# Experts of a hybrid decoder: token transposes moved behind the product transposes, and one filler matmul per pair of experts

## The chip, the cores and the metric

The kernel runs on one core of one Trainium2 chip. The metric is the device time of one execution in microseconds (us), and lower is better. Everything is float32.

## The reference, cut to what matters

The program is one inference step of a two-layer trunk with 320 tokens (256 of a prompt, 64 of a sample) of width 1024. Layer 0 mixes tokens with a Mamba-2 scan, layer 1 with latent attention. Behind either mixer stands the same mixture of experts, and the change lies in that alone. Each token goes to 2 of 32 experts, and each expert is a SwiGLU of width 256:

```python
for g in range(MOE_GROUPS):
    sl = slice(g * EXPERTS_PER_GROUP, (g + 1) * EXPERTS_PER_GROUP)
    hg = jax.nn.silu(jnp.einsum('nd,edf->nef', xt, w_gate[sl])) * jnp.einsum('nd,edf->nef', xt, w_up[sl])
    hg = hg * gate[:, sl, None].astype(hg.dtype)
    out = out + jnp.einsum('nef,efd->nd', hg, w_down[sl], preferred_element_type=jnp.float32)
```

The kernel computes each expert only for the tokens routed to it, and applies the two weights of a token afterwards.

## The kernel before

**Pairs.** The 32 experts of a layer are worked on as 16 pairs (`PAIRS`), numbered by j. Each expert has 64 slots for tokens, so a pair fills 128 rows. If an expert has more than 64 tokens, the whole loop over pairs would run again (a "window"); here it runs once a layer.

**One pair, step by step.** GpSimd gathers the 128 token rows of pair j from DRAM (`gather`, L1208). TensorE transposes them, 8 blocks of 128x128, into two PSUM banks (`turn`, L1072). ScalarE copies the first four blocks to SBUF (`rows_in` of ScalarE, L1158) and VectorE the other four (`rows_in` of VectorE, L1399). TensorE multiplies them with the gate and up weights of both experts (`gate_up`, L1086: 32 matmuls of 64 output rows, the two experts side by side). ScalarE takes SiLU of the gate half (`silu`, L1164), and VectorE multiplies it with the up half (`hidden`, L1406). TensorE transposes that product (`turn_hidden`, L1096, two blocks), VectorE copies it to `hT` (`hidden_turned`, L1411), and TensorE multiplies it with the down weights (`down`, L1111: 16 matmuls). ScalarE and VectorE copy the result out (L1170, L1417), and GpSimd scatters it to DRAM (`scatter`, L1216).

**The order on TensorE** is written out by hand and runs ahead of itself. Turn j of the loop holds filler matmuls, `gate_up(j + 1)`, `turn(w, j + 2)`, `turn_hidden(j)` and `down(j)`. The filler is `idle_work(n, bank)` (L1013): n matmuls of a constant 128x512 block that nobody reads. In the rows of a trace a float32 matmul counts as two records.

**The order on VectorE** follows it: in turn j, `hidden(j + 1)`, `rows_in(j + 2)`, `hidden_turned(j)`, `rows_out(w, j)`. An engine works its own list strictly in order, so an instruction that waits for a semaphore holds up all behind it.

**The weights.** A pair has 6 MB of weights, and there are six slots of one expert each (`RING`; in the trace four are called `ring` and two `hi`), so three pairs. SyncE issues all these loads into one DMA queue: gate and up weights of a pair (L211, 2 MB an expert) as soon as `gate_up` of three pairs before is done, the down weights (L216, 1 MB an expert) as soon as its `down` is done. Pairs 0 to 2 are loaded while the mixer and the router still work. `gate_up(j)` waits until both experts' loads have landed, `down(j)` likewise.

Of the kernel before, what the change touches and what calls it, by code (L numbers as in the profile page):

```python
# [141 lines left out]
def program(nc, a, o):  # L142
    ctx = ExitStack()
    with ctx:
# [674 lines left out]
        def expert_layer(layer, afterwards):  # L819


            with ExitStack() as st:
# [39 lines left out]
                def slot(i):  # L862
                    return ring[:, i % RING, :] if i % RING < 4 else hi[:, i % RING - 4, :]
# [16 lines left out]
                LG, POS, MAP, COUNT, HT = (4, 4, 5), 5, 5, 2, 4  # L880
# [7 lines left out]
                def load_windows(eng):  # L888
                    eng.wait_ge(windows_set, 1)
                    return eng.value_load(windows[0:1, 0:1], min_val=1, max_val=MAX_WINDOWS)  # L890

                def meet(eng, w):

                    eng.wait_ge(go, w + 1)
                    eng.sem_inc(passed, 1)
# [113 lines left out]
                def _(pe):  # L1009
                    def idle_work(n, bank):  # L1010

                        for _ in range(n):
                            pe.matmul(ps[:, bank, :], ident, C[:, 0:512], start=True, stop=True)  # L1013
# [39 lines left out]
                    def slot_map():  # L1053

                        pe.wait_ge(ids_made, 1)
                        for k in range(2):
                            for t in range(NT):
                                mm = pe.matmul(ps[:, MAP, 256:256 + 2 * PAIRS], onehot[:, k, t, :],
                                               ids[:, k, t, :, :].rearrange("p c j -> p (c j)"),
                                               start=(k + t == 0), stop=(k == 1 and t == NT - 1))  # L1060
                        mm.then_inc(map_done, 1)

                    def turn(w, j):
                        p = j % 2
                        pe.wait_ge(xs_in[p], PER_WINDOW * w + 16 * (j // 2) + 16)
                        if j:
                            pe.wait_ge(xs_act, j)
                            pe.wait_ge(xs_dve, j)
                        for half in range(2):
                            for k in range(4):  # L1070
                                at = (4 * half + k) * P
                                tr = pe.transpose(ps[:, TP[half], k * P:(k + 1) * P], xs[:, p, at:at + P], ident)  # L1072
                            tr.then_inc(turned, 1)

                    def gate_up(j):
                        p = j % 2
                        pe.wait_ge(xs_act, j + 1)
                        pe.wait_ge(xs_dve, j + 1)
                        for i in (2 * j, 2 * j + 1):
                            pe.wait_ge(gate_up_in[i % RING], 16 * (i // RING) + 16)  # L1080
                        if j >= 2:
                            pe.wait_ge(h_done, j - 1)
                        for k in range(KD):
                            for e in range(2):
                                w = slot(2 * j + e)[:, 0:2 * KD * FF].rearrange("p (g k f) -> p g k f", g=2, k=KD)
                                mm = pe.matmul(ps[e * SLOTS:(e + 1) * SLOTS, GU[p], :].rearrange("p (g f) -> p g f", g=2),  # L1086
                                               xsT[:, p, k, e * SLOTS:(e + 1) * SLOTS], w[:, :, k, :],
                                               start=(k == 0), stop=(k == KD - 1))
                        mm.then_inc(gu_done, 1)

                    def turn_hidden(j):
                        pe.wait_ge(h_done, j + 1)
                        if j:
                            pe.wait_ge(ht_copied, j)
                        for f in range(2):
                            tr = pe.transpose(ps[:, HT, f * P:(f + 1) * P], hid[:, j % 2, f * P:(f + 1) * P], ident)  # L1096
                        tr.then_inc(ht_done, 1)

                    def down(j):
                        p = j % 2  # L1100
                        pe.wait_ge(ht_copied, j + 1)
                        for i in (2 * j, 2 * j + 1):
                            pe.wait_ge(down_in[i % RING], 16 * (i // RING) + 16)
                        if j:
                            pe.wait_ge(y_act, j)
                            pe.wait_ge(y_dve, j)
                        for m in range(2):
                            for f in range(2):
                                for e in range(2):
                                    at = 2 * KD * FF + f * D + m * 512  # L1110
                                    mm = pe.matmul(ps[e * SLOTS:(e + 1) * SLOTS, YB[m], :],  # L1111
                                                   hT[:, p, f, e * SLOTS:(e + 1) * SLOTS],
                                                   slot(2 * j + e)[:, at:at + 512], start=(f == 0), stop=(f == 1))
                        mm.then_inc(d_done, 1)

                    n_windows = pe.alloc_register(f"windows_pe{layer}")
                    with pe.Fori(0, n_windows) as w:
                        slot_map()
                        idle_work(4, 7)
                        turn(w, 0)  # L1120
                        gate_up(0)
                        turn(w, 1)
                        for j in range(PAIRS):
                            if j + 1 < PAIRS:
                                idle_work(2, MAP)
                                gate_up(j + 1)
                            if j + 2 < PAIRS:
                                turn(w, j + 2)
                            turn_hidden(j)
                            down(j)  # L1130
                        pe.reg_mov(n_windows, load_windows(pe))
                        pe.wait_ge(d_done, PAIRS)
                        pe.sem_inc(arrived, 1)
                        meet(pe, w)
# [105 lines left out]
                def _(v):  # L1240
# [105 lines left out]
                    def indices(each):  # L1346

                        found = ps[:, MAP, 256:256 + 2 * PAIRS].rearrange("p (c j) -> p c j", c=2)
                        v.wait_ge(map_done, 1)
                        each.mark(v.tensor_scalar(empty[:, :, :], found, 0.5, 4.0 * NSLOT, ALU.is_lt, ALU.mult))  # L1350
                        each.settle(v)
                        v.scalar_tensor_tensor(out=index[:, :, :], in0=found, scalar=-1.0, in1=empty[:, :, :],  # L1352
                                               op0=ALU.add, op1=ALU.add).then_inc(index_set, 1)
# [49 lines left out]
                    def hidden(j):  # L1403
                        p = j % 2
                        v.wait_ge(silu_done, j + 1)
                        v.tensor_tensor(hid[:, p, :], sg[:, p, :], ps[:, GU[p], FF:2 * FF], ALU.mult).then_inc(h_done, 1)  # L1406

                    def hidden_turned(j):
                        p = j % 2
                        v.wait_ge(ht_done, j + 1)  # L1410
                        v.tensor_copy(hT[:, p, :, :], ps[:, HT, 0:2 * P].rearrange("p (f s) -> p f s", f=2)).then_inc(ht_copied, 1)  # L1411
# [8 lines left out]
                    with v.Fori(0, n_windows) as w:  # L1420
                        each = Tally(win_dve)
                        slot_columns(each)
                        indices(each)
                        count_windows(each)
                        rows_in(0)
                        with v.If(w < 1):
                            once = Tally(dve)
                            once.loop(step.base + step.n)
                            combine_weights(once)
                            residual(once)  # L1430
                        hidden(0)
                        rows_in(1)
                        for j in range(PAIRS):
                            if j + 1 < PAIRS:
                                hidden(j + 1)
                            if j + 2 < PAIRS:
                                rows_in(j + 2)
                            hidden_turned(j)
                            rows_out(w, j)
                        v.reg_mov(n_windows, load_windows(v))  # L1440
                        v.wait_ge(y_dve, PAIRS)
                        v.sem_inc(arrived, 1)
                        meet(v, w)
# [711 lines left out]
```

## Time and profile before

| what | us |
|---|---|
| median of 3 runs | 1538.79 (1537.5 to 1547.11) |
| the profiled execution, its own time | 1550.08 |
| its span, first to last instruction | 1548.2 |
| TensorE busy | 1313.0 (85% of the span) |
| TensorE weight loads busy | 709.8 |
| VectorE, ScalarE, GpSimd busy | 457.7, 240.6, 130.8 |
| `gate_up` (L1086) and `down` (L1111) matmuls from `ring` | 157.5 and 80.4 |
| filler matmuls, L1013 | 94.4 |

All times in the rows are counted from the span's first instruction. The time of an execution is its span and 1.9 us around it. "GB/s" is what all 16 DMA engines moved. PEclk is the clock that TensorE was granted, as a share of 2.4 GHz. "Busy" of TensorE holds matmuls of the filler too, so a busy TensorE alone does not say what the kernel waits for.

### The profile page before, as it was taken

What the parts mean: (1) busy time and instruction counts of PE and PEld (TensorE: products, weight loads), DVE (VectorE), ACT (ScalarE), POOL (GpSimd) and SP (SyncE); (2) the same over time, 40 slices, a digit from 0 to 9 for tenths busy, and PEclk for the clock granted to TensorE, in tenths of its full rate; (3) what the DMA queues carried; (4) which work ended last, traced back from release to release, by engine and by line L of the source; (5) the groups of instructions that cost most, each with busy time, mean ns of one, the idle gap of its engine ahead of it and who ended that gap; (6) DMA issues with size and microseconds to landing.
All of it is one profiled execution on the core that took longest, in us unless ns stands there. A gap on an engine that the chain in (4) does not pass through costs nothing. (4 is left out here: it accounts for less than half of the span.)

```text
span 1548.2 us, 14859 instructions
## 1 busy us (share of the span) xinstructions
PE 1313.0 (85%) x5208; PEld 709.8 (46%) x5208; DVE 457.7 (30%) x1209; ACT 240.6 (16%) x570; POOL 130.8 (8%) x191
## 2 busy tenths in 40 slices
PE   7999956669987999989898488779998989989881
PEld 4777645456653335333333245546655353333330
DVE  0057744434344016211211523221110153121114
ACT  0101112110002002111111213221101121111111
POOL 0000013330000000111110000000000000111100
PEclk9999957655558998999999689696657979999996
DMA  5323540002412436999994730504424358999953
GB/s 232 110 109 118 210 169 1 28 1 82 163 64 89 163 135 238 397 422 424 423 421 173 267 132 1 173 11 123 123 61 190 141 233 356 422 421 423 418 216 111
DMA packets 53199, 309.36 MB, mean 200 GB/s; under 512 B 12754, under 2 KB 17746, under 8 KB 31250
## 3 DMA queue, kind: packets, MB, share of 16 engines
q1 hardware_dynamic: 43186, 295.42, 48.1%
q0 software_dynamic: 9216, 10.51, 2.0%
q10 hardware_dynamic: 736, 2.62, 0.5%
q8 instruction: 37, 0.61, 0.2%
q14 instruction: 24, 0.20, 0.0%
HBM read 300.61 MB, written 30.97 MB: 214 GB/s over the span
## 5 line engine op out<-in xcount | busy, mean ns | idle before, releaser
L294 PE MATMUL ps<-XT,ring 128*128 128x320 f32 x640 | 175.4, 438 | 11.2 <-DMA ring<-in_w_in 11.2
L1086 PE MATMUL ps<-ring,xsT 128*64 128x512 f32 x704 | 157.5, 600 | 3.0 <-ACT xsT L1158 3.0
L294 PEld LDWEIGHTS ps<-XT,ring 128*128 128x128 f32 x640 | 123.4, 193 | 62.8 <-issue 13.2
L1111 PE MATMUL ps<-ring,hT 128*64 128x512 f32 x352 | 80.4, 599 | 33.1 <-DVE hT L1411 33.1
L1086 PEld LDWEIGHTS ps<-ring,xsT 128*64 128x64 f32 x704 | 50.2, 138 | 106.7 <-issue 101.7
L1013 PE MATMUL ps<-C 128*128 128x512 f32 x184 | 94.4, 646 | 0.0
L1406 DVE TENSOR_TENSOR work<-work,ps 128x256 f32<-128x256 f32 x32 | 13.5, 421 | 257.7 <-ACT work L1164 257.7
L814 PE MATMUL ps<-ring,zT 128*128 128x512 f32 (+1 forms) x192 | 87.8, 605 | 0.0
L1086 PE MATMUL ps<-hi,xsT 128*64 128x512 f32 x320 | 70.9, 596 | 0.0
L1216 POOL DMA_INDIRECT y_dram<-ys,index x32 | 32.1, 1004 | 407.0 <-DVE ys L1417 407.0
L1208 POOL DMA_INDIRECT XT<-x_dram,index x32 | 32.5, 1017 | 358.1 <-DVE index L1352 326.3
L1111 PEld LDWEIGHTS ps<-ring,hT 128*64 128x64 f32 x352 | 23.3, 137 | 76.1 <-DVE hT L1411 38.4
L1417 DVE COPY ys<-ps 128x512 f32<-128x512 f32 x32 | 22.1, 691 | 121.5 <-PE ps L1111 121.5
L1013 PEld LDWEIGHTS ps<-C 128*128 128x128 f32 x184 | 34.1, 202 | 52.1 <-issue 51.9
L713 PE MATMUL ps<-ring,Bm 64*128 64x512 f32 x64 | 57.5, 1078 | 0.0
L814 PEld LDWEIGHTS ps<-ring,zT 128*128 128x128 f32 (+1 forms) x192 | 30.6, 172 | 56.7 <-issue 56.6
L522 PE MATMUL ps<-seg,ring 128*64 128x128 f32 (+1 forms) x192 | 23.2, 368 | 36.7 <-DVE seg L581 36.7
L1158 ACT ACTIVATE xsT<-ps,gb 128x128 f32<-128x128 f32 x128 | 48.1, 455 | 39.3 <-PE ps L1072 39.3
L1164 ACT ACTIVATE work<-ps 128x256 f32<-128x256 f32 x32 | 12.3, 384 | 264.5 <-PE ps L1086 264.5
L1261 DVE SCALAR_TENSOR_TENSOR X<-X,ps 128x1024 f32<-128x1024 f32 (+1 forms) x6 | 7.3, 1211 | 146.5 <-PEq L751 79.1
L1111 PE MATMUL ps<-hi,hT 128*64 128x512 f32 x160 | 36.5, 599 | 14.4 <-DVE hT L1411 14.4
L1399 DVE TENSOR_SCALAR xsT<-ps,gb 128x128 f32<-128x128 f32 x128 | 43.7, 403 | 14.6 <-PE ps L1072 14.6
(292 smaller groups left out, 1686.9 us busy)
## 6 DMA issues: line engine op xcount, KB each, us to landing
ring<-in_experts SPq DMA_DIRECT2D x44, 2048.0 KB, 16.1
ring<-in_experts SPq DMA_DIRECT2D x44, 1024.0 KB, 15.8
hi<-in_experts SPq DMA_DIRECT2D x20, 2048.0 KB, 16.3
ring<-in_w_in SPq DMA_DIRECT2D x10, 2048.0 KB, 8.0
hi<-in_experts SPq DMA_DIRECT2D x20, 1024.0 KB, 17.7
ring<-in_latent SPq DMA_DIRECT2D x48, 256.0 KB, 2.8
ring<-in_w_out SPq DMA_DIRECT2D x4, 2048.0 KB, 12.8
ring<-in_state SPq DMA_DIRECT2D x4, 1024.0 KB, 6.9
```

The lines of the kernel that those rows point to most:

```text
L294: mm = pe.matmul(ps[:, q, 0:TOK], ring[:, u, k * 512 + q * P:k * 512 + (q + 1) * P], XT[:, k, :], start=(k == 0), stop=(k == KD - 1))
L522: mm = pe.matmul(out, xdt[0:r, h * HP:(h + 1) * HP], seg[0:r, u % 2, j, 0:r], start=True, stop=not carried)
L713: pe.matmul(ps[:, UP[g], :], Bm[:, b % 2, g * STATE:(g + 1) * STATE], xdtw[0:64, g * 512:(g + 1) * 512], start=True, stop=True).then_inc(u ...
L814: mm = pe.matmul(ps[0:ROWS[t], 2 * t + n, :], zT[:, blk, OFF[t]:OFF[t] + ROWS[t]], ring[:, blk // 4, at:at + 512], start=(blk == 0), stop= ...
L1013: pe.matmul(ps[:, bank, :], ident, C[:, 0:512], start=True, stop=True)
L1086: mm = pe.matmul(ps[e * SLOTS:(e + 1) * SLOTS, GU[p], :].rearrange("p (g f) -> p g f", g=2), xsT[:, p, k, e * SLOTS:(e + 1) * SLOTS], w[:, ...
L1111: mm = pe.matmul(ps[e * SLOTS:(e + 1) * SLOTS, YB[m], :], hT[:, p, f, e * SLOTS:(e + 1) * SLOTS], slot(2 * j + e)[:, at:at + 512], start=( ...
L1158: ins = act.activation(xsT[:, j % 2, k, :], ps[:, TP[0], k * P:(k + 1) * P], ACT.Identity, bias=gb[:, 0, 1, k:k + 1], scale=gb[:, 0, 0, k: ...
L1208: pool.indirect_dma_start(out=xs[:, j % 2, :], out_offset=None, in_=x_dram, in_offset=bass.IndirectOffsetOnAxis(ap=index[:, 0, j:j + 1], a ...
L1216: pool.indirect_dma_start(out=y_dram, out_offset=bass.IndirectOffsetOnAxis(ap=index[:, 1, j:j + 1], axis=0), in_=ys[:, j % 2, :], in_offse ...
L1399: ins = v.tensor_scalar(xsT[:, j % 2, k, :], ps[:, TP[k // 4], k % 4 * P:(k % 4 + 1) * P], gb[:, 0, 0, k:k + 1], gb[:, 0, 1, k:k + 1], ALU ...
L1417: v.tensor_copy(ys[:, j % 2, 512:D], ps[:, YB[1], :]).then_inc(y_dve, 1)
```

## The change

In the list of TensorE, the token transposes `turn(w, j + 2)` and the product transposes `turn_hidden(j)` change places, so that the token transposes stand between the product transposes and `down(j)`. In the list of VectorE, `hidden_turned(j)` and `rows_in(j + 2)` change places in the same way. The lists of ScalarE, GpSimd and SyncE stay as they are. Ahead of each `gate_up(j + 1)` stands one filler matmul where there were two.

```diff
@@ -1122,11 +1122,11 @@
                         turn(w, 1)
                         for j in range(PAIRS):
                             if j + 1 < PAIRS:
-                                idle_work(2, MAP)
+                                idle_work(1, MAP)
                                 gate_up(j + 1)
+                            turn_hidden(j)
                             if j + 2 < PAIRS:
                                 turn(w, j + 2)
-                            turn_hidden(j)
                             down(j)
@@ -1433,9 +1433,9 @@
                         for j in range(PAIRS):
                             if j + 1 < PAIRS:
                                 hidden(j + 1)
+                            hidden_turned(j)
                             if j + 2 < PAIRS:
                                 rows_in(j + 2)
-                            hidden_turned(j)
                             rows_out(w, j)
```

## Rows read from the trace of the kernel before

**Rows 1.** Windows, layer 0: length, busy us of each engine, PEclk, DMA share, GB/s

```profile
800.20:815.60 15.40, 13.83 (x65) 5.02 (x63) 2.81 (x8) 2.48 (x7) 2.02 (x2) 1.00 1.01 419
...
620.30:833.50 213.20, 191.16 (x862) 70.60 (x864) 41.27 (x103) 36.05 (x88) 26.31 (x26) 1.00 0.98 410
```

**Rows 2.** Timeline, one turn: start, duration, engine, line, operation, [idle before <-releaser]

```profile
744.32 1.99 PE L1013 MATMUL ps<-C 128*128 128x512 f32 x4
...
746.23 7.09 PE L1086 MATMUL ps<-ring,xsT 128*64 128x512 f32 x32
...
753.25 1.09 PE L1072 MATMUL ps<-C,XT 128*128 128x128 f32 x8
...
753.78 0.42 DVE L1406 TENSOR_TENSOR work<-work,ps 128x256 f32<-128x256 f32 x1 [8.66 <-ACT work L1164]
...
754.18 0.38 PE L1096 MATMUL ps<-C,work 128*128 128x128 f32 x2
754.38 1.37 DVE L1399 TENSOR_SCALAR xsT<-ps,gb 128x128 f32<-128x128 f32 x4 [0.18 <-PE ps L1072]
755.66 0.42 DVE L1411 COPY hT<-ps 128x256 f32<-128x256 f32 x1
...
756.14 3.65 PE L1111 MATMUL ps<-hi,hT 128*64 128x512 f32 x16 [1.58 <-DVE hT L1411]
...
759.72 1.98 PE L1013 MATMUL ps<-C 128*128 128x512 f32 x4
```

**Rows 3.** Timeline, layer 0's first filler and what stands beside it

```profile
621.57 1.35 DVE L1399 TENSOR_SCALAR xsT<-ps,gb 128x128 f32<-128x128 f32 x4
...
623.02 7.09 PE L1086 MATMUL ps<-ring,xsT 128*64 128x512 f32 x32
```

**Rows 4.** Timeline of SyncE: issues of pair 4's gate/up, 15's, 15's down, layer 1's 15's

```profile
630.14 0.80 SPq L211 DMA_DIRECT2D ring<-in_experts  x2
...
799.56 0.81 SPq L211 DMA_DIRECT2D ring<-in_experts  x2
...
821.43 0.81 SPq L216 DMA_DIRECT2D ring<-in_experts  x2
...
1461.30 0.80 SPq L211 DMA_DIRECT2D ring<-in_experts  x2
```

**Rows 5.** DMA view, second issue of each of those four: count, KB, us to landing

```profile
ring<-in_experts SPq DMA_DIRECT2D x1, 2048.0 KB, 15.5
...
ring<-in_experts SPq DMA_DIRECT2D x1, 2048.0 KB, 23.9
...
ring<-in_experts SPq DMA_DIRECT2D x1, 1024.0 KB, 13.1
...
ring<-in_experts SPq DMA_DIRECT2D x1, 2048.0 KB, 24.7
```

**Rows 6.** Timeline, the last `gate_up` (pair 15) of layer 0 and of layer 1

```profile
838.63 7.09 PE L1086 MATMUL ps<-ring,xsT 128*64 128x512 f32 x32
...
1500.37 7.09 PE L1086 MATMUL ps<-ring,xsT 128*64 128x512 f32 x32
```

**Rows 7.** Pair 15's gather and transposes, timeline; landing of gathers issued at 654.8 and 808.8

```profile
808.83 1.02 POOL L1208 DMA_INDIRECT XT<-x_dram,index  x1 [0.30 <-issue]
...
830.25 1.09 PE L1072 MATMUL ps<-C,XT 128*128 128x128 f32 x8
...
XT<-x_dram,index POOLq DMA_INDIRECT x1, 11.1
...
XT<-x_dram,index POOLq DMA_INDIRECT x1, 14.5
```

**Rows 8.** Timeline and windows, layer 1's first `gate_up` behind idle stretches and transposes

```profile
1273.39 8.70 PE L1086 MATMUL ps<-ring,xsT 128*64 128x512 f32 x32 [1.51 <-ACT xsT L1158]
...
1273.40:1276.70 3.30, 3.30 (x8) 1.09 (x10) 3.16 (x8) 0.00 (x0) 0.00 (x0) 0.51 0.18 45
```

## Prediction

> **What bounds the kernel now.** I began with the windows of the expert loop. In a turn of 15.40 us TensorE is busy for 13.83 us at full clock, and the DMA engines are busy throughout [rows 1]. Both look like the bound, so the timeline of one turn and the landings of the weights have to decide.
>
> The timeline shows TensorE's turn from filler to filler: 744.32 to 759.72, so 15.40 us. It holds two filler matmuls (1.91 us until `gate_up` starts), `gate_up` (7.02 us until the next operation starts), token transposes (0.93), product transposes, 1.57 us idle, and `down` (3.58 until the next filler) [rows 2]. TensorE waits only once, for VectorE's copy to `hT`. That copy ends at 756.08, since VectorE does the four copies of token blocks (754.38 to 755.75) ahead of it. TensorE never waits for weights. So TensorE sets the pace today.
>
> The landings show how far behind the weights are. Pair 4's second load, issued 0.4 us after the row's start at 630.14, needs 15.5 us and lands at 646.0. Pair 15's, issued at 799.96, needs 23.9 us and lands at 823.9 [rows 4, 5]. The loads of a pair thus come (823.9 - 646.0) / 11 = **16.17 us** apart, slower than TensorE's 15.40 us. It doesn't show yet because the loop starts with three pairs in the slots: `gate_up(15)` starts at 838.63 [rows 6], 14.7 us after its weights. From 620.3 to 833.5 the DMA engines are busy for 0.98 of the time [rows 1], so these landings can't come earlier by issuing earlier: the queue always holds work.
>
> **The change part by part.**
>
> *One filler fewer.* Two take 1.91 us [rows 2], so one gives back **0.95 us** a turn. In turn 0 it gives nothing: `gate_up(1)` starts at 623.02, and VectorE's copies for it end only at 622.92 [rows 3]. Fourteen turns remain ahead of `gate_up(15)`.
>
> *The exchange on TensorE and VectorE.* Let `gate_up(j + 1)` end at E = 753.25. The product transposes of pair j need `hid` of pair j, which was made one turn earlier, so they run at E and not at E + 0.93. VectorE makes `hid` of pair j + 1 until 754.20 (E + 0.95) [rows 2]. The copy to `hT` now follows it at once: 0.42 us and 0.03 between them, so it ends at E + 1.40, and `down` started 0.06 us behind it before (756.08 to 756.14), so now at E + 1.46. The token transposes, 0.28 + 0.93 us, are done at E + 1.21 and lie beside it. `down` started at E + 2.89. The exchange gives **1.43 us** a turn, in turns 0 to 13 (turn 14 has no later pair to transpose). What moves back on VectorE is the copy of pair j + 2's blocks, by some 0.4 us; it is needed by `gate_up(j + 2)`, behind all of `down` and a filler, so I cost it at nothing. ScalarE's four copies wait 0.3 us longer for the token transposes, with the same cover. The banks and `hT` are free long before, for each pair's `down` ends before the next product transposes. GpSimd issues a gather behind the scatter of the pair before, so it starts earlier with `down`, see below. On SyncE no load is moved past another; they are issued earlier, into a queue that isn't empty.
>
> *What TensorE could do.* Its turn shrinks to 15.40 - 1.43 - 0.95 = 13.02 us. It could start `gate_up(15)` at 838.6 - 14 x 2.38 = 805.3.
>
> *What is late next.* The weights of pair 15 land at 823.9. Counted back, TensorE is ready for pair 15 - n at 805.3 - 13.02 n and its weights are there at 823.9 - 16.17 n; the two meet at n = 5.9. So pairs 3 to 9 run free, and from pair 10 on each `gate_up` waits for its loads: 3.15 us of idle TensorE a turn, behind the filler. The start of `gate_up(15)` moves from 838.63 to 824.0, a gain of **14.6 us**. What follows it is unchanged in length; the last down weights, issued at 821.83 and landed after 13.1 us at 834.9 [rows 4, 5], are needed some 12 us after 824.0, and can't be later with the same full queue. In layer 1 the last gate and up loads land at 1461.70 + 24.7 = 1486.4, and `gate_up(15)` started at 1500.37 [rows 4 to 6]: a gain of **13.9 us**. Of the 33.3 us that TensorE gives a layer, less than half reaches the time.
>
> *Traffic.* By 824 us one more scatter will have passed through the same engines. From nothing to 0.4 us a layer; I take 0.35, **-0.7 us** in all. It is the small part of the wait for a gather [rows 7] that its own bytes can fill at the rate of the windows [rows 1].
>
> *The clock.* Before, the longest idle stretch in a turn was 1.57 us and the clock stayed at 1.00. Now there are stretches of 3.15 us. The nearest row is layer 1's first `gate_up`: behind stretches of waiting with only transposes between them it ran for 8.70 us where all others take 7.09, and the granted clock was 0.51 in that stretch [rows 8], so at the 1.2 GHz level. A fall costs 1.61 us there and was over within that one `gate_up`. In the middle of the paced pairs a fall costs nothing: TensorE is then later by 1.6 us and idles 1.5 us instead of 3.15. Only a fall ahead of `gate_up(15)` counts. Bounds are 0 and 1.6 us a layer; the phase is open, so I count it in one layer: **-1.6 us**.
>
> The Trainium skill ("TensorE: Matmul & The Clock Gate", section on HAM oscillation) says that a wait for a DMA between bursts of matmuls brings the engine back to its low clock, in each round of the loop. By that rule taken strictly both layers pay it, and the sum would be 1.6 us worse. The short idle stretches of this trace don't test it.
>
> *The sum:* 14.6 + 13.9 - 0.7 - 1.6 = **26.2 us**. Against the profiled execution of 1550.08 us that gives 1523.9; it lies 11.3 us over the median of the runs shown, and taken from that median, 1538.79, it gives **1512.6 us**, or 1.7% less.
>
> **The rivals.**
>
> *A. As above*, the weights pace the last six pairs: 1505 to 1522 us, the spread of the runs before (1537.5 to 1547.11) and the clock's bounds included. Chance 0.74.
>
> *B. The weights come faster than their landings say.* Saturated windows move 419 GB/s and more, and the mean of the whole stretch is 410 [rows 1]; landings tell of the last of 16 engines, and in the tail some are idle already. If the engines even out, 2% of 213 us, some 5 us a layer, come on top, about 1503 us; with the one layer's fall of the clock absent, about 1501. With no limit by weights at all it would be 33.3 us a layer, 1472 us, against which the 16.17 us speak. Chances 0.08 and 0.02.
>
> *C. The clock costs more.* It falls ahead of `gate_up(15)`, and comes back only by its end: 7 us instead of 1.6, in one or both layers, 1518 to 1527 us. Chance 0.06.
>
> *D. Gathers become late.* A gather is issued 2.9 us behind `down(j)` and is needed by the transposes of pair j + 4; pair 15's landed at 808.8 + 14.5 = 823.3, with 6.9 us to spare [rows 7]. Their time grew from 11.1 to 14.5 us while the weights' grew from 15.5 to 23.9 us. In the new order the weight queue is up to 41 us deep (`gate_up(9)` ends at 805.3 - 6 x 13.02 + 7.02 = 734, which issues pair 12's loads; they land at 823.9 - 3 x 16.17 = 775); at the same slope of 0.4 a gather would take some 21 us. Two turns are then the gather and 7.4 us (issue, token transposes, `down`), so it limits from 25 us on. At 28 us a turn lasts 17.7 us, five turns lose 8 us a layer, and the time is near 1528. For it speaks the growth, against it that it has 4 us too much to go. Chance 0.04.
>
> The Trainium skill ("DMA: Bandwidth & Descriptors", section on queues, rings and completion order) says that each DMA engine takes turns between its queues, so a deeper weight queue should not delay a gather. By that alone the gathers would stay near 12 us and D fall away; the trace, with 11.1 to 14.5, doesn't quite agree.
>
> *E. Slower than before: the clock stays low once the waits begin.* At 1.2 GHz the matmuls of a turn (7.02 + 3.58 + 0.95) and 1.2 us of transposes take twice as long, and the turn is 25.8 us. From pair 10, whose weights land at 743, five such turns put `gate_up(15)` at 872 instead of 838.6: 33 us a layer, some 1605 us. It decides from (838.6 - 743) / 5 = 19.1 us a turn, a loss of 6.1 us, nearly four times the 1.61 of the row. Against it: a TensorE slower than the weights no longer waits, and what lowered the clock is gone. Chance 0.04.
>
> *F. No effect*, because `down` is released by something that I don't see, such as the loads' order; chance 0.02.
>
> **How the numbers follow.** The forecast is A's. B's first case, 1501 less the 3 us by which runs scatter, and C's fill the range: 1498 to 1526 us; outside are B's second case, E and F, and ends of C and D. One per cent, about what can be told from no change, is 15.4 us, so the bound lies at 1523.4. Faster by more: A, B and half of C, 0.87. Within: the rest of C, D and F, 0.08. Slower: E and a little besides, 0.05.
>
> **What would show it.** In turns 1 to 7: filler to filler near 13.0 us, one filler pair of records, the product transposes ahead of the token transposes, `down` 1.46 us behind `gate_up`'s end, no wait for a DMA. From about pair 10: `gate_up` idle some 3 us with the DMA of `in_experts` as releaser, turns of 16.2 us. Loads issued earlier, with landings up to 41 us, and the last of them at the same distance from the loop's start as before. The granted clock below 1.00 in single windows of that half only. The prediction is wrong if pair 15's weights land more than 7 us earlier or later in the loop than before, if turns before pair 8 wait for anything, or if the clock is low over several turns.

## The result and the profile after

| | before | after |
|---|---|---|
| median of 8 executions each, us | 1545.17 (1537.5 to 1562.11) | 1524.44 (1518.87 to 1536.14) |
| ratio, with its 95% interval | | 0.9899 (0.9849 to 0.9948) |
| the profiled execution | 1550.08 | 1536.14 |
| all executions of the study, mean | 1548.4 (63) | 1522.9 (20) |

The forecast was 1512.6 us, 26.2 us less than the kernel before. The change is faster, by 1.0% in this comparison, and the forecast was 11.8 us below the measured median. Over all executions of either kernel that this study ran, the difference is 25.5 us (with some 5 us of uncertainty, from standard deviations of 8.7 and 9.4 us), a ratio of 0.9835. These executions come from several chips. In the three sessions that ran both kernels side by side the means differ by 23.2, 30.5 and 27.1 us. One execution of the kernel before, of 3166 us, is left out.

The ratios leave out executions that are over 1.5% above the fastest of their kernel, which in the first comparison dropped three of before (1561.5 to 1562.1 us) and none of after, and so made the gain look smaller than the medians show.

The stage table comes from one windows view of each kernel, cut at the start of layer 0's `gate_up(0)`, its `gate_up(15)`, layer 1's `gate_up(0)`, its `gate_up(15)`, and the end. The columns are as in [rows 1]. First the kernel before:

```profile
613.17:838.63 225.46, 203.41 (x912) 74.89 (x912) 48.92 (x115) 36.65 (x89) 26.62 (x27) 1.00 0.93 388
838.63:1273.39 434.76, 366.05 (x1352) 216.01 (x1351) 107.22 (x314) 87.80 (x237) 11.38 (x30) 0.78 0.37 130
1273.39:1500.37 226.98, 204.96 (x913) 74.62 (x913) 49.08 (x115) 36.66 (x89) 26.60 (x27) 0.99 0.93 385
1500.37:1548.20 47.83, 15.13 (x69) 4.72 (x68) 18.41 (x26) 7.67 (x14) 2.60 (x3) 0.73 0.29 93
```

Then the kernel after:

```profile
610.73:823.52 212.79, 196.97 (x883) 72.92 (x883) 48.96 (x115) 36.64 (x89) 26.31 (x26) 0.97 0.97 403
823.52:1271.08 447.56, 377.96 (x1352) 219.20 (x1351) 107.21 (x314) 87.74 (x237) 11.70 (x30) 0.76 0.37 130
1271.08:1484.80 213.72, 196.74 (x882) 72.58 (x883) 49.12 (x115) 36.65 (x89) 27.26 (x27) 0.97 0.96 401
1484.80:1534.30 49.50, 16.83 (x68) 5.63 (x68) 18.41 (x26) 7.67 (x14) 1.94 (x2) 0.68 0.36 125
```

The two expert loops went from 225.46 and 226.98 us to 212.79 and 213.72: **25.9 us** less, which is the effect of the change. The stretch between them, which the change doesn't touch, took 12.8 us longer in this profile, at a granted clock of 0.76 instead of 0.78, and the end 1.7 us longer. The start, up to the first loop, was 2.4 us shorter.

A free turn of the timeline answers to [rows 2]:

```profile
659.58 7.09 PE L1086 MATMUL ps<-ring,xsT 128*64 128x512 f32 x32
...
666.60 0.44 PE L1096 MATMUL ps<-C,work 128*128 128x128 f32 x2
...
666.87 1.04 PE L1072 MATMUL ps<-C,XT 128*128 128x128 f32 x8
667.13 0.42 DVE L1406 TENSOR_TENSOR work<-work,ps 128x256 f32<-128x256 f32 x1 [7.70 <-ACT work L1164]
667.47 0.42 DVE L1411 COPY hT<-ps 128x256 f32<-128x256 f32 x1
...
667.94 3.65 PE L1111 MATMUL ps<-ring,hT 128*64 128x512 f32 x16
667.95 1.37 DVE L1399 TENSOR_SCALAR xsT<-ps,gb 128x128 f32<-128x128 f32 x4
...
671.52 1.13 PE L1013 MATMUL ps<-C 128*128 128x512 f32 x2
```

`gate_up` ends at 666.60. `down` starts 1.34 us behind it, where it was 2.89, and has no idle time of its own. The forecast was 1.46: it let the copy to `hT` start 0.45 us behind the start of VectorE's product, and it starts 0.34 us behind it (667.13 to 667.47). (The x32 and x16 are records. The kernel issues 16 matmuls for `gate_up` and 8 for `down`, two records each; the description of a pair gives the records as matmuls.) VectorE's token copies now begin when `down` does. From 658.52, the filler before, to 671.52 the turn is 13.00 us.

From pair 9 on the rows look different. These are `gate_up(9)` to `gate_up(11)`, then `gate_up(14)` and `(15)`, of layer 0:

```profile
727.35 8.78 PE L1086 MATMUL ps<-ring,xsT 128*64 128x512 f32 x32 [2.70 <-DMA ring<-in_experts]
743.45 7.09 PE L1086 MATMUL ps<-ring,xsT 128*64 128x512 f32 x32 [1.34 <-DMA ring<-in_experts]
759.46 8.48 PE L1086 MATMUL ps<-hi,xsT 128*64 128x512 f32 x32 [2.96 <-DMA hi<-in_experts]
...
807.61 10.00 PE L1086 MATMUL ps<-hi,xsT 128*64 128x512 f32 x32 [2.97 <-DMA hi<-in_experts]
...
823.52 7.09 PE L1086 MATMUL ps<-ring,xsT 128*64 128x512 f32 x32
```

From `gate_up(9)` to `gate_up(14)` the starts are 16.0 to 16.1 us apart, the releaser is the weights' DMA, and behind some of the waits `gate_up` takes 8.5 to 10 us for its 7.09. The last one, `gate_up(15)`, has no wait: the slow `gate_up(14)` ahead of it made TensorE itself the later of the two. The pages of the two kernels say the same of the chain that ended last, before and after. The DMA leads it now, together with TensorE, where TensorE's 15% did:

```profile
PE 15%; DVE 3%; DMA 1%; ACT 1%; issue 0%; SPq 0%; POOLq 0%; another core or an unknown queue 0%; DVEq 0%
```

```profile
DMA 8%; PE 8%; DVE 2%; ACT 1%; issue 0%; SPq 0%; POOLq 0%; another core or an unknown queue 0%; DVEq 0%
```

The weights' landings answer to [rows 5]. First the second gate and up load of pair 15 in layer 0, its issue and its time to landing, so it landed at 822.7:

```profile
783.01 1.54 SPq L211 DMA_DIRECT2D ring<-in_experts  x1
...
ring<-in_experts SPq DMA_DIRECT2D x1, 2048.0 KB, 39.7
```

Over all L211 issues (min, median, max), and then the same for the gathers of L1208, of [rows 7]:

```profile
DMA to landing us min/median/max: 7.2/25.9/41.4
```

```profile
DMA to landing us min/median/max: 3.3/13.4/15.8
```

The queue of weights got as deep as forecast (41 us), and the gathers hardly noticed: before, their median was 12.2 us and their maximum 14.9.

### The profile page after: what moved, and what is told of

Same layout as the page of the kernel before. It is cut to its first block and busy times, and to the rows that moved or that the text cites. A ratio compares the mean times of both kernels' runs of the same rounds, so it can differ in the third digit from the quotient of the medians.

```text
span 1534.3 us, 14739 instructions
## 1 busy us (share of the span) xinstructions
PE 1309.0 (85%) x5148; PEld 707.7 (46%) x5148; DVE 459.0 (30%) x1209; ACT 240.5 (16%) x570; POOL 130.7 (9%) x191
## 5 line engine op out<-in xcount | busy, mean ns | idle before, releaser
L1086 PE MATMUL ps<-ring,xsT 128*64 128x512 f32 x704 | 165.0, 623 | 27.3 <-DMA ring<-in_experts 22.8
L294 PE MATMUL ps<-XT,ring 128*128 128x320 f32 x640 | 174.3, 436 | 11.3 <-DMA ring<-in_w_in 11.3
L1086 PEld LDWEIGHTS ps<-ring,xsT 128*64 128x64 f32 x704 | 56.1, 143 | 133.3 <-issue 126.7
L1406 DVE TENSOR_TENSOR work<-work,ps 128x256 f32<-128x256 f32 x32 | 13.4, 420 | 276.7 <-ACT work L1164 276.7
L1086 PE MATMUL ps<-hi,xsT 128*64 128x512 f32 x320 | 75.2, 625 | 7.8 <-DMA hi<-in_experts 7.8
L1013 PE MATMUL ps<-C 128*128 128x512 f32 x124 | 68.6, 671 | 0.0
L1208 POOL DMA_INDIRECT XT<-x_dram,index x32 | 32.5, 1017 | 357.8 <-DVE index L1352 326.2
L814 PEld LDWEIGHTS ps<-ring,zT 128*128 128x128 f32 (+1 forms) x192 | 30.5, 172 | 56.8 <-issue 56.6
L1158 ACT ACTIVATE xsT<-ps,gb 128x128 f32<-128x128 f32 x128 | 48.1, 455 | 45.4 <-PE ps L1072 45.4
L1086 PEld LDWEIGHTS ps<-hi,xsT 128*64 128x64 f32 x320 | 24.5, 144 | 57.5 <-issue 57.5
L1935 PE MATMUL ps<-ring 128*128 128x64 f32 x192 | 42.5, 413 | 4.7 <-ACT ring L1997 4.7
```

The source lines that it names most:

```text
L294: mm = pe.matmul(ps[:, q, 0:TOK], ring[:, u, k * 512 + q * P:k * 512 + (q + 1) * P], XT[:, k, :], start=(k == 0), stop=(k == KD - 1))
L814: mm = pe.matmul(ps[0:ROWS[t], 2 * t + n, :], zT[:, blk, OFF[t]:OFF[t] + ROWS[t]], ring[:, blk // 4, at:at + 512], start=(blk == 0), stop= ...
L1158: ins = act.activation(xsT[:, j % 2, k, :], ps[:, TP[0], k * P:(k + 1) * P], ACT.Identity, bias=gb[:, 0, 1, k:k + 1], scale=gb[:, 0, 0, k: ...
L1208: pool.indirect_dma_start(out=xs[:, j % 2, :], out_offset=None, in_=x_dram, in_offset=bass.IndirectOffsetOnAxis(ap=index[:, 0, j:j + 1], a ...
L1935: pe.matmul(out, lat(n, i)[:, c * P:(c + 1) * P], pTs[b][:, i * 64:(i + 1) * 64], start=(i == 0), stop=False)
```

## The experiments

Each kernel ran side by side with the kernel before on one chip, but not all of them on the same chip. "Loops" are the stretches from `gate_up(0)` to `gate_up(15)` in layers 0 and 1, "between" the stretch from there to layer 1's `gate_up(0)`, and "end" what follows the last `gate_up(15)`; all from one profile each. One execution of no_filler, of 3926 us, counts in its median and not in its ratio.

| kernel | loops, us | between | end | median | ratio to before (95%) |
|---|---|---|---|---|---|
| before | 225.5, 227.0 | 434.8 | 47.8 | 1545.17 | |
| before_again | 225.5, 227.1 | 427.7 | 48.1 | 1549.28 | 1.0025 (0.9991 to 1.006) |
| after | 212.8, 213.7 | 447.6 | 49.5 | 1524.44 | 0.9899 (0.9849 to 0.9948) |
| after_again | 212.3, 214.2 | 427.2 | 50.2 | 1514.53 | 0.9804 (0.9764 to 0.9844) |
| after_third | 212.4, 213.6 | 430.5 | 48.4 | 1523.59 | 0.9822 (0.976 to 0.9883) |
| exchange_only | 212.2, 213.8 | 430.5 | 47.3 | 1516.91 | 0.9859 (0.9815 to 0.9904) |
| filler_only | 213.5, 214.9 | 446.6 | 49.0 | 1525.19 | 0.9831 (0.9774 to 0.9887) |
| no_late_down | 191.9, 193.3 | 423.9 | 47.4 | 1483.99 | 0.9634 (0.9593 to 0.9675) |
| late_fillers | 212.2, 213.9 | 427.2 | 47.7 | 1524.76 | 0.9789 (0.9737 to 0.984) |
| no_filler | 212.3, 213.9 | 430.4 | 48.1 | 1524.98 | 0.9878 (0.9829 to 0.9926) |
| attention_fillers | 211.7, 214.4 | 428.3 | 48.0 | 1512.7 | 0.9794 (0.9754 to 0.9835) |
| three_fillers | 212.1, 214.0 | 417.0 | 47.6 | 1504.02 | 0.973 (0.9695 to 0.9764) |
| four_fillers | 212.3, 212.3 | 429.7 | 47.8 | 1506.8 | 0.9744 (0.9704 to 0.9784) |

### Each half of the change alone

```diff
# exchange_only, against the kernel after
-                                idle_work(1, MAP)
+                                idle_work(2, MAP)
# filler_only, against the kernel before
-                                idle_work(2, MAP)
+                                idle_work(1, MAP)
```

> The exchange alone, two fillers as before. Theory (weights set the end of the loop): a free turn of TensorE is 13.95 us, gate_up(15) could start 20.0 us earlier than before and its weights come 12 to 14 us earlier, so gate_up(0) to gate_up(15) is 212 to 214 us in layer 0, the same as with the full change; waits for weights of some 2 us from about pair 13 on, the granted clock 1.00 nearly throughout the loop; time equal to the full change within 3 us. Rival (both halves count in the end): the loop takes 217 to 219 us and the kernel is 9 us slower than the full change.

> One filler fewer, the order as before. Theory (weights set the end of the loop): a free turn is 14.45 us, fourteen of them bring gate_up(15) 13.3 us forward, about where its weights land: gate_up(0) to gate_up(15) is 212 to 213.5 us in layer 0, with hardly a wait for weights and no fall of the clock; time equal to the full change within 3 us or some us better. Rival (both halves count): 219 to 221 us, 14 us slower than the full change.

Either half alone gives nearly the whole loop: 212.2 us and 213.5 us, where the change has 212.8. The free turns were 13.86 us (forecast 13.95) and 14.54 us (14.45). The means of all their executions, 1521.8 us (11) and 1523.4 us (6), can't be told from the change's 1522.9 us. This is the mark of a second bound close behind the first: the second half of an improvement buys hardly anything. The two stop for different reasons, though. With the exchange alone the last four `gate_up` of layer 0 wait for the weights, 1.9 to 2.3 us each. With one filler fewer alone no `gate_up` waits for weights: the first turn of 9.86 us and fourteen of 14.54 make 213.4 us, so TensorE still sets the end of that loop, and happens to reach it less than 2 us behind the weights. The windows of layer 0's loop, exchange_only and then filler_only:

```profile
611.23:823.48 212.25, 203.69 (x912) 76.18 (x913) 49.00 (x115) 36.73 (x89) 27.39 (x27) 1.00 0.97 404
```

```profile
606.71:820.19 213.48, 190.55 (x882) 69.14 (x883) 48.94 (x115) 36.74 (x89) 26.40 (x26) 1.00 0.97 403
```

The granted clock is 1.00 in layer 0's loop for both, where the change has 0.97. Waits of 2 us can lower it all the same: in exchange_only `gate_up(15)` of layer 0 took 8.79 us behind a wait of 2.03 us, at a mean granted clock of 0.80, and `gate_up(12)` of layer 1 took 8.79 behind one of 2.20.

### A third of the weights' bytes taken away

```diff
# no_late_down, against the kernel after
                                     sp.wait_ge(d_done, j - 3)
-                                    for i in (2 * j - 2, 2 * j - 1):
-                                        load_down(sp, layer, i, slot(i))
...
                         for i in (2 * j, 2 * j + 1):
-                            pe.wait_ge(down_in[i % RING], 16 * (i // RING) + 16)
+                            pe.wait_ge(down_in[i % RING], 16)
```

> The changed kernel without the loads of the down weights of pairs 3 to 15 (these pairs multiply with old ones), which is a third of the weights' bytes. Theory (weights set the end of the loop): loads of a pair then take some 10.7 us, all turns are 13.0 us, no gate_up waits, the clock stays 1.00; gate_up(0) to gate_up(15) is 192 us in each layer, and the time is some 41 us below the full change. Rival (something else paces pairs 10 to 15): turns of 16 us remain, 213 us, and the time is the full change's.

The loops are 191.9 and 193.3 us, every turn but the first is 13.00 us, and no `gate_up` waits for a DMA. The mean of its executions is 1484.8 us, 38 below that of the change. So it is the loads of the weights that hold back TensorE from pair 9 on.

```profile
612.92:804.78 191.86, 190.54 (x883) 69.13 (x883) 48.99 (x115) 36.66 (x89) 26.32 (x26) 1.00 0.80 314
```

TensorE is busy for 190.5 of 191.9 us, and the DMA share is 0.80 where the change has 0.97.

### What the fillers do in the waits

```diff
# late_fillers, against the kernel after
-                                idle_work(1, MAP)
+                                idle_work(4 if j >= 8 else 1, MAP)
# no_filler, against the kernel after
-                                idle_work(1, MAP)
```

> The changed kernel with four fillers instead of one ahead of gate_up(9) to gate_up(15), where TensorE waits for weights. Theory (the waits are 3.1 us, and they lower the clock): three more fillers take 2.85 us of each wait, gate_up starts when it did, no fall of the clock in the loop; gate_up(0) to gate_up(15) stays 212 to 214 us, and the stretch from layer 1's gate_up(15) to the end, 49.5 and 50.2 us in the two profiles of the change, goes back to the 47.3 to 47.8 us of the kernels without such a fall; in all 2 to 5 us less than the change. Rival (clock falls in the waits are hidden in the next wait): no difference.

> The changed kernel with no filler in the loop. Theory: a free turn is 12.05 us, weights pace from about pair 8, waits of 4.0 us each; the loop ends where it did, 212 to 215 us, and the clock falls in more of the waits (about every second pair or more), which costs at most some 3 us at the end of each layer. Rival (the fillers hold the clock, without them it is lost): turns of TensorE of 18 us and more at 1.2 GHz, a loop over 230 us, slower than the change by 30 us or more.

Four fillers in the waits keep the clock at 1.00 and 0.99 and the loops at 212.2 and 213.9 us. No filler lets it fall to means of 0.95 and 0.94, and the loops are 212.3 and 213.9 us. Layer 0's loop, late_fillers and then no_filler:

```profile
611.28:823.48 212.20, 208.99 (x924) 79.30 (x925) 48.99 (x115) 36.74 (x89) 27.39 (x27) 1.00 0.97 404
```

```profile
611.80:824.13 212.33, 183.80 (x852) 70.72 (x853) 48.96 (x115) 36.72 (x89) 27.39 (x27) 0.95 0.97 404
```

So within the loop the clock costs nothing: a late `gate_up` only shortens the next wait. Without fillers the free turns were 11.79 us (forecast 12.05), and the waits began at pair 7 (forecast about 8).

What the clock can cost is the last `gate_up` of a layer, which has no wait behind it. In the first profile of the change, in layer 1:

```profile
1484.80 8.78 PE L1086 MATMUL ps<-ring,xsT 128*64 128x512 f32 x32 [2.30 <-DMA ring<-in_experts]
```

The granted clock over this row is 0.81. It took 8.78 or 8.79 us in two profiles of the change, with ends of 49.5 and 50.2 us. In the third it took 7.09, as with late fillers and without fillers, with ends of 48.4, 47.7 and 48.1 us. In layer 0 it took 7.09, 8.79 and 8.78 us in the three profiles of the change; that time falls into the stretch between the loops. So the 1.7 us are met or missed by chance, in either layer. Not all of an end's length is this: filler_only had 49.0 us with a `gate_up(15)` of 7.09. The 2 to 5 us less that late_fillers was expected to give can't be seen: the mean of its executions is 1523.9 us, against 1522.9 for the change.

### The same kernels again

> The changed kernel unaltered, profiled once more. Theory (the experts' gain is whole, the rest lies in the attention between them): from gate_up(0) to gate_up(15) of a layer again 212.8 and 213.7 us within 1.5 us (before: 225.5 and 227.0), while the stretch from layer 0's gate_up(15) to layer 1's gate_up(0), 434.8 us before and 447.6 in the first profile of the change, comes out elsewhere in that range, with a granted clock that goes with it. Rival (the earlier end of the experts does something fixed to the attention): that stretch is 447.6 us again, within 1 us.

> The kernel before, unaltered, against itself: what the comparison tells from no change, and a second profile. Theory: ratio 1.00 with an interval of half a per cent or so, single medians up to 10 us apart; loops of 225.5 and 227 us again, and a stretch between layer 0's gate_up(15) and layer 1's gate_up(0) that differs from 434.8 us by several us. Rival: that stretch is fixed at 434.8 for this kernel, within 1 us.

> The changed kernel unaltered, a third profile and more executions. Theory: loops of 212 to 214 us once more, six samples of the sample attention in two lengths only, 17.25 and 20.5 us, in whatever mixture; the mean of all its executions lies 24 to 28 us below that of the kernel before, a ratio of 0.982 to 0.985. Rival (the first comparison was right, the second lucky): a ratio of 0.99.

The loops repeat within 0.6 us. The stretch between them doesn't: 447.6, 427.2 and 430.5 us for the change, 434.8 and 427.7 for the kernel before. So the 12.8 us that the first profile lost are no fixed effect of the change. The kernel before against itself gives 1.0025 (0.9991 to 1.006).

Of the 12.8 us, 11.2 lie in the sample attention, which works on eight samples one after the other. Most of these samples have one of two lengths. The windows below hold six samples, from a mark of the second to the same mark of the eighth, and then the last of the six. In the first profile of the change:

```profile
1028.41:1149.71 121.30, 116.57 (x381) 64.68 (x379) 18.16 (x48) 15.07 (x48) 4.28 (x18) 0.59 0.35 98
...
1129.23:1149.71 20.48, 19.69 (x66) 11.04 (x64) 3.02 (x8) 2.57 (x8) 0.00 (x0) 0.58 0.10 29
```

In its second:

```profile
1019.63:1123.11 103.48, 98.75 (x380) 59.45 (x379) 18.16 (x48) 15.06 (x48) 4.28 (x18) 0.70 0.39 115
...
1105.86:1123.11 17.25, 16.46 (x65) 10.29 (x64) 3.03 (x8) 2.57 (x8) 0.00 (x0) 0.70 0.22 68
```

In the kernel before:

```profile
1041.81:1151.92 110.11, 105.38 (x381) 62.26 (x379) 18.14 (x48) 15.06 (x48) 4.28 (x18) 0.66 0.37 108
```

The same instructions take 17.25 us a sample at a granted clock of 0.70, or 20.5 us at 0.58, and once a sample is in one of these patterns, most of the following keep it (the change's first profile: 18.9 and five of 20.5; its second: six of 17.25; before: four of 17.26, two of 20.54; the change's third and before_again: five of 17.25, one of 20.50). Six samples took 103.5, 106.7, 110.1 or 121.3 us. Nothing in these samples was changed. The executions without a detailed trace fit this: over 55 of the kernel before, the mean granted clock goes against the time with a correlation of -0.97, from 1534.9 us at 0.858 to 1564.0 us at 0.839.

### Fillers in the sample attention

```diff
# attention_fillers, against the kernel after
                         pe.wait_ge(pt_copied, n + 1)
                         for c in range(2):
+                            pe.matmul(ps[:, TB, :], ident, C[:, 0:512], start=True, stop=True)
# three_fillers: late_fillers, the lines above, and
                         pe.sem_inc(passed, 1)
+                        pe.matmul(ps[:, TB, :], ident, C[:, 0:512], start=True, stop=True)
                         for i in range(PAGES):
# four_fillers: late_fillers, the lines of attention_fillers, and
                             for i in range(PAGES):
+                                if i == 5:
+                                    pe.matmul(ps[:, TB, :], ident, C[:, 0:512], start=True, stop=True)
```

> The changed kernel with two filler matmuls of 512 columns per sample in the sample attention (L1935), one ahead of each group of nine narrow matmuls. Theory (the 12 us that the first profile of the change lost between the layers are clock: the sample attention runs at 1.2 GHz for 10 us of 17 before and for 17 of 20.5 after): with the fillers it runs at 2.4 GHz, a sample takes some 15.8 us with both fillers in it, the stretch between the layers is 405 to 425 us, and the time is 5 to 30 us below the change. Rival (the clock there doesn't depend on what stands in the loop): each filler adds 1 to 2 us, so the stretch is 16 to 30 us longer.

> late_fillers with three fillers per sample in the sample attention: one ahead of the transposes of the probabilities and one ahead of each group of nine narrow matmuls. Theory (the length of a sample follows the granted clock, 14.2 us with two fillers at 2.4 GHz and 20.7 when it falls): with the third filler a sample takes 15.2 us and the clock falls more rarely; the six samples take 91 to 100 us where they took 103.5 to 121 in profiles of the change, so the time is 5 to 20 us below the change and scatters less. Rival (two fillers were enough to see all there is): samples of 15.2 and 21.7 us mixed as before, no gain over the change.

> late_fillers with four fillers per sample, one ahead of each group of nine narrow matmuls and one within each group, behind its fifth. Theory: 16.1 us a sample at 2.4 GHz with no fall at all, 97 us for six samples, a scatter between executions of 10 us and less, and a time 5 to 20 us below the change. Rival: the clock falls all the same and each filler only costs; samples of 17 to 23 us, slower than the change.

With two fillers a sample takes 14.20 us (forecast 15.8), with both fillers in it, when the clock is 1.00; but in that profile two of the six still took 20.7 us and one 15.9:

```profile
1021.25:1121.03 99.78, 95.05 (x405) 54.63 (x403) 18.16 (x48) 15.05 (x48) 4.28 (x18) 0.85 0.42 119
```

The stretch between the layers was 428.3 us, above the 405 to 425 expected, and the median 1512.7. With three fillers all six samples take 15.26 us at 1.00. The second window is the whole stretch between the layers:

```profile
1022.44:1113.98 91.54, 86.81 (x416) 46.65 (x415) 18.16 (x48) 15.07 (x48) 4.34 (x18) 1.00 0.45 130
```

```profile
823.16:1240.16 417.00, 347.80 (x1399) 198.17 (x1399) 107.30 (x314) 87.89 (x237) 10.78 (x29) 0.88 0.40 139
```

Its timeline shows what the full clock does to the narrow matmuls, the x16 rows of 64 columns. First such a row of the kernel before, 3.67 us at a granted clock of 0.50, then three_fillers, 1.89 us at 1.00:

```profile
1064.44 3.67 PE L1935 MATMUL ps<-ring 128*128 128x64 f32 x16
```

```profile
1040.56 1.13 PE L1934 MATMUL ps<-C 128*128 128x512 f32 x2 [0.79 <-ACT ring L1999]
1041.53 1.89 PE L1937 MATMUL ps<-ring 128*128 128x64 f32 x16
```

This is the fastest kernel of the study: 1504.02 us (1501.49 to 1508.59), ratio 0.973, and its executions lie within 7 us, where those of the change spread over 31. On the chip that ran both, the means are 1504.5 and 1525.1 us. It also holds the late fillers, which alone gave nothing (above). Four fillers, none of them ahead of the transposes, gave 15.92 us for five samples and 19.15 for one, so the expected "no fall at all" was missed, and 1506.8 us. It isn't shown whether the third filler helps by its number or by its place.

## Why the prediction was right in its steps and off in its number

*TensorE sets the pace, and the weights are close behind.* Right, and the core of it: no_late_down removes the wait, and the exchange alone already meets it.

*The filler gives 0.95 us and the exchange 1.43 us a turn.* Together 2.38 forecast and 2.40 measured (15.40 to 13.00). Split otherwise: 0.86 us for the filler and 1.54 for the exchange, by the free turns of 14.54 and 13.86. Half of 1.91 us was no fair price for one filler: with one left, `gate_up` starts 1.06 us behind its start (658.52 to 659.58). The first turn of layer 0 gained nothing (9.86 us before and after), as read from [rows 3].

*Weights 16.17 us apart, waits from pair 10 of 3.15 us.* In layer 0 pair 4's second load landed at 645.0 and pair 15's at 822.7, so 16.15 us apart. The waits came from pair 9, of 2.7 to 3.0 us in layer 0 where no late `gate_up` shortens them; in layer 1 they began with 1.9 us, and one was of 3.9.

*Gains of 14.6 and 13.9 us in the loops.* Measured 12.7 and 13.3 in the first profile, and in the other two 13.2 and 12.8, 13.1 and 13.4. The term was 1.4 to 1.9 us too large in layer 0, mostly because pair 15's weights were later: its second load landed at 783.01 + 39.7 = 822.7, or 212.0 us behind the start of `gate_up(0)`, against 210.7 before. In the first profile `gate_up(15)` then started 0.8 us behind that landing, without a wait, held up by the slow `gate_up(14)`. The term for traffic, 0.35 us a layer, had the right sign and was too small. The 1.3 us don't grow along the loop: pair 4's second load already landed 34.3 us behind `gate_up(0)` against 32.8 before. Up to pair 15's landing the queues moved 85.6 MB against 84.7. Of the 0.9 MB more, 0.14 are gathers and scatters, or 0.35 us at 404 GB/s, which is the term; the rest is in the weights' queue, which has the same loads ahead of pair 15 in both kernels. So it would be loads behind pair 15's, issued earlier now and sharing the engines with it. No run isolates this.

*The clock, 1.6 us in one layer.* In the first profile it fell behind three waits of either layer. One of those in layer 1 was ahead of the last `gate_up`, where it cost 1.7 us (49.5 for 47.8), and one in layer 0 held up `gate_up(15)` by at most 0.8 us. In the second profile both layers paid the 1.7 us, in the third layer 0 alone. Waits for the weights' DMA did bring the clock down, behind some of them in the first profile (2.3 to 3.9 us) and not behind others (3.00 and 3.01 us). The Trainium skill ("TensorE: Matmul & The Clock Gate", section on HAM oscillation) has such a fall in each round of the loop; the traces agree with it in part. Mostly `gate_up` then took 8.5 to 8.8 us for its 7.09, as in [rows 8]; at 807.61 it took 10.00 and at 1453.40 9.67. That such losses don't add up is shown by no_filler. Rival C had the clock's cost at 7 us a layer, and that didn't occur. That the median of 1524.44 us lies in its range (1518 to 1527), and outside A's (1505 to 1522), is chance.

*Rival D, late gathers.* They took 15.8 us at most against a forecast of 21, with the weights at 41 us. The rule of the Trainium skill in "DMA: Bandwidth & Descriptors", section on queues, rings and completion order, fits these numbers better than my slope of 0.4 did, although a maximum of 15.8 is still more than the 14.9 before.

*The sum of 26.2 us.* The loops gave 25.9, less 1.7 at the end in the first profile; all executions together give 25.5. That it fits so well is in part luck, for its 27.8 us from the loops (14.6 + 13.9 - 0.7) were 1.3 to 1.9 us too many, and the clock's cost came out between 1.7 and 3.4 us. The difference of the first two medians is only 20.7 us, for the reason that follows.

**What failed is the last step:** "it lies 11.3 us over the median of the runs shown, and taken from that median, 1538.79, it gives **1512.6 us**". I took a median of three for the level of the kernel, although the profiled execution stood 11 us above it. The mean of 63 is 1548.4 us, 9.6 us above that base; from it the same sum gives 1522.2, and the measured mean of the change is 1522.9. So the mechanism and the gain held, and the base, with the untouched stretch taken as of one length, did not. The trace had the warning: [rows 1] show the clock of the loop, where nothing wavers, and I didn't look at the 435 us between the loops, where it has a mean of 0.78 and where samples of the same work stood in the timeline with 17.26 and 20.54 us. The range, 1498 to 1526, should have taken in that scatter of the base, which no term of it does.

## What to carry to other kernels

- When the next bound lies 15 us behind the present one, read it from landings, not from busy shares, and don't pay for the second half of a change: in layer 0's loop the halves gave 13.2 and 12.0 us, and both together 12.7 to 13.2.
- A stretch that the change doesn't touch still has to be looked at. Where its repeated units have two lengths, the time is drawn anew in every execution (1534.9 to 1564.0 us for the kernel before), and a median of three can't tell 1%.
- Compare stages between profiles before explaining a total. A difference in an untouched stage that a second profile doesn't repeat is no fixed effect of the change.

## What I had not expected of the hardware

- The same sample of attention has two lengths that repeat, 17.25 us at a granted clock of 0.70 and 20.5 us at 0.58, with TensorE busy for 16.5 and 19.7 us of them.
- A TensorE that is busy for 95% of the time may still be granted half its clock: with samples at a mean granted clock of 0.58 and 0.70, its narrow matmuls, 64 columns, took 3.67 us for the 1.89 at full clock, and the granted clock over that row is 0.50, so 1.2 GHz. Three matmuls of 512 columns a sample, 3 us of work that nobody reads, made a sample 2.0 to 5.2 us shorter (15.26 us), at 2.4 GHz throughout.
- A weight queue 41 us deep delayed gathers in another queue by only some 1 us in the median (12.2 to 13.4 us).
